# Four heads written out, another order at the heads' ends, and finer waits around the output projection, in a hybrid block on one core

## The reference

```python
def mlstm_branch(...):
    xc = jax.nn.silu(causal_conv(xm, conv_w, conv_b))
    q, k = heads(xc) @ w_q, (heads(xc) @ w_k) * MLSTM_HEAD_DIM ** -0.5
    v = heads(xm) @ w_v
    h = mlstm_chunkwise(q, k, v, i_pre, logf)
    h = jax.nn.sigmoid(heads(z)) * h
    mu, var = mean(h), mean((h - mu) ** 2)          # over the 384 of a head
    h = (h - mu) * lax.rsqrt(var + EPS)
    h = h * mh_gain + skip * xc
    return h @ w_proj
...
    merged = jax.nn.sigmoid(g_a) * y_a + jax.nn.sigmoid(g_b) * y_b
    h = h + merged @ w_out[l]
    h = h + peer(rmsnorm(h, norm2_g[l]), w_query[l], ...)
```

## Time and profile before

| | us |
|---|---|
| median of 3 runs | 4103.37 (4101.56 to 4104.65) |
| the profiled execution | 4104.21 |
| its span, first to last instruction | 4102.7 |
| PE busy | 3998.3 (97%) |
| DVE, ACT, POOL busy | 2465.8, 1239.6, 939.0 |
| granted clock of the PE, mean | 0.990 |
| a matmul of 128x128 by 128x512, mean (2048 of them, L1889) | 0.391 |

### The profile page before, as it was taken

One profiled execution on the slowest core, in us unless ns is written; L12 is line 12 of the kernel. 1 busy time (PEld: TensorE's weight loads), 2 busy tenths in 40 slices (PEclk: granted clock), 3 DMA queues, 4 the chain that ended last, 5 costly groups with the idle time before them and its releaser, 6 DMA issues.

```text
span 4102.7 us, 54068 instructions
## 1 busy us (share of the span) xinstructions
PE 3998.3 (97%) x19149; PEld 3450.3 (84%) x19149; DVE 2465.8 (60%) x3452; ACT 1239.6 (30%) x1313; POOL 939.0 (23%) x679
## 2 busy tenths in 40 slices
PE   8999999988999899999999999999999999999997
PEld 5887777776778688888888888888899999999997
DVE  7556777466532745454666664222247887888884
ACT  4333232333222422222333332222222222222223
POOL 3100000421111254545000000000014444444432
PEclk9999999999999999999999999999999999999999
DMA  4643333642543445455777778666768888888883
GB/s 173 197 140 123 127 123 113 228 151 77 179 146 115 165 157 183 159 183 187 229 252 239 243 238 307 218 216 215 228 225 301 322 301 313 306 308 323 303 321 127
DMA packets 239995, 867.64 MB, mean 211 GB/s; under 512 B 22680, under 2 KB 61096, under 8 KB 172224
## 3 DMA queue, kind: packets, MB, share of 16 engines
q1 hardware_dynamic: 96576, 454.07, 30.5%
q10 hardware_dynamic: 94080, 204.49, 16.2%
q0 software_dynamic: 49280, 208.36, 14.4%
HBM read 768.25 MB, written 232.81 MB: 244 GB/s over the span
## 4 chain that ended last, share of the span: by engine, by line
PE 50%; DVE 6%; DMA 5%; issue 3%; ACT 2%; DVEq 1%; SPq 0%; ACTq 0%
PE mm L1889 12%; PE mm L1890 12%; PE mm L1891 12%; DMA raw<-stream 5%; DVE wlo L1101 2%; PE pv L1889 2%; PE pv L1890 2%; PE pv L1891 2%; DVE acc L1813 2%; PE sc L1891 1%; PE sc L1890 1%; PE sc L1889 1%; ACT whi L673 1%; ACT actb L1009 1%; DVE gl L1788 1%
## 5 line engine op out<-in xcount | busy, mean ns | idle before, releaser
L1101 DVE TENSOR_TENSOR wlo<-raw,whi 128x2048 fp32r<-128x2048 f32 x331 | 759.2, 2294 | 773.3 <-ACT whi L673 763.6
L673 ACT ACTIVATE whi<-raw 128x2048 fp32r<-128x2048 f32 x380 | 727.5, 1914 | 493.0 <-issue 194.2
L1889 PE MATMUL mm<-t_hi,whi 128*128 128x512 f32 x2048 | 800.0, 391 | 7.5 <-DVE t_lo L1618 3.9
L1890 PE MATMUL mm<-t_lo,whi 128*128 128x512 f32 x2048 | 798.0, 390 | 0.0
L1891 PE MATMUL mm<-t_hi,wlo 128*128 128x512 f32 x2048 | 797.6, 389 | 0.0
L1889 PEld LDWEIGHTS mm<-t_hi,whi 128*128 128x128 f32 x2048 | 385.1, 188 | 90.5 <-DVE t_lo L1618 8.1
L1891 PEld LDWEIGHTS mm<-t_hi,wlo 128*128 128x128 f32 x2048 | 384.7, 188 | 80.7
L1890 PEld LDWEIGHTS mm<-t_lo,whi 128*128 128x128 f32 x2048 | 385.1, 188 | 77.6
L1889 PE MATMUL mm<-hn_hi,whi 128*128 128x512 f32 x960 | 377.4, 393 | 4.6 <-DVE wlo L1101 4.6
L1890 PE MATMUL mm<-hn_lo,whi 128*128 128x512 f32 x960 | 374.3, 390 | 0.0
L1891 PE MATMUL mm<-hn_hi,wlo 128*128 128x512 f32 x960 | 373.8, 389 | 0.0
...
## 6 DMA issues: line engine op xcount, KB each, us to landing
...
ev_d<-stream ACTq DMA_DIRECT2D x128, 1024.0 KB, 6.1
up_d<-sgl ACTq DMA_DIRECT2D x128, 256.0 KB, 2.1
...
gg<-g_d SPq DMA_DIRECT2D x15, 1536.0 KB, 12.2
gl<-up_d SPq DMA_DIRECT2D x120, 192.0 KB, 5.1
...
```

Of the source, the lines that this page charges most:

```text
L673: act.activation(whi[:, k, :], raw[:, k, :], ACT.Copy).then_inc(hi_done, 1)
L1101: dve.tensor_tensor(wlo[:, k, :], raw[:, k, :], whi[:, k, :].bitcast(F32), ALU.subtract)\
L1889: pe.matmul(out, lh, rh, start=start, stop=False)
L1890: pe.matmul(out, lh, rl, start=False, stop=False)
```

## The change

Heads: all four are written out on every engine, with no loop. DVE writes the divided sums to a new buffer `gh`, which POOL gates in place; the centring reads `gh` and writes `hh`. So a head's tail now spreads over two heads: the mean, centring, squares and root of head h-1 in head h; its gain, skip and halves in head h+1. The low half is written by POOL (`finished_low`), for the last head by DVE. DVE does both units' `wlo` and the Newton step ahead of the division. The PE does `qk(4)` ahead of the mean, and the squares after `value(1)`. The third square has a buffer of its own (`hs2`). POOL issues `m_bc` and `gcol` before the gating, `em_bc` after it, beside `sz`.

Before the heads: within the GLU loop POOL loads four instead of eight late blocks of `xc`; the others go in one piece behind the first `xm`.

Roots: one `Abs_reciprocal_sqrt` in place of Ln and Exp, in all places; the Newton step stays.

Output projection: its first tile waits for 15 merged blocks, and for the 16th only at its end. The last tile signals each block, on which ScalarE writes `t_hi`; DVE does 13 blocks of `t_lo` before the last residual. The sum of squares goes into the first query tile, before its sixth block.

```diff
-        gcol = S("gcol", [P, TB], F32, 200)
+        gcol = S("gcol", [P, TB], F32, 207.25)
+        gh = S("gh", [P, HC, T], F32, 152)
+        hs2 = S("hs2", [P, T], F32, 200)
...
-        hsq = (hs[:, 0, :], hs[:, 1, :], pf[:, 0, :])
+        hsq = (hs[:, 0, :], hs[:, 1, :], hs2[:])
...
-                c = MC - KC // 2 + p
-                load_conv(1, slice(c, c + 1))
+                if p < HC + 1:
+                    load_conv(1, slice(HC + 1 + p, HC + 2 + p))
...
+            def finished_low(h):
+                for c in range(HC):
+                    pool.wait_ge(hfhi_done, 3 * h + c + 1)
+                    pool.tensor_tensor(xc_lo[:, 3 * h + c, :], hh[:, c, :], xc_hi[:, 3 * h + c, :].bitcast(F32),
+                                       ALU.subtract).then_inc(hflo_done, 1)
...
-            def head(h, first, last):
-                if not first:
-                    z_gate(h - 1)
-                    pool.wait_ge(en_done, 4 * h)
-                    pool.wait_ge(pv_free, 3 * h)
-                    pool.dma_start(m_bc[:], gates_d[1, h].partition_broadcast(P)).then_inc(bcst_in, 16)
-                    pool.dma_start(em_bc[:], gates_d[2, h].partition_broadcast(P)).then_inc(bcst_in, 16)
-                    with nc.allow_non_contiguous_dma(reason="one value a partition"):
-                        pool.dma_start(gcol[:], gates_d[0, h].rearrange("(s p) -> p s", p=P)).then_inc(bcst_in, 16)
+            def next_gates(h):
+                pool.wait_ge(en_done, 4 * h)
+                pool.dma_start(m_bc[:], gates_d[1, h].partition_broadcast(P)).then_inc(bcst_in, 16)
+                with nc.allow_non_contiguous_dma(reason="one value a partition"):
+                    pool.dma_start(gcol[:], gates_d[0, h].rearrange("(s p) -> p s", p=P)).then_inc(bcst_in, 16)
+            def next_sz(h):
                 pool.wait_ge(hz_done, 3 * h)
                 pool.dma_start(sz[:], z_heads[h]).then_inc(sz_in, 16)
-                if not first:
-                    skips(h - 1, (0, 1))
-                if not last:
+                if h:
+                    pool.wait_ge(pv_free, 3 * h)
+                    pool.dma_start(em_bc[:], gates_d[2, h].partition_broadcast(P)).then_inc(sz_in, 16)
+            next_xm(0)
+            load_conv(1, slice(MC - HC - 1, MC))
+            next_sz(0)
+            next_xm(1)
+            for h in range(1, HEADS):
+                next_gates(h)
+                z_gate(h - 1)
+                next_sz(h)
+                if h >= 2:
+                    skips(h - 2, (2,))
+                    finished_low(h - 2)
+                if h < HEADS - 1:
                     next_xm(h + 1)
-                if not first:
-                    skips(h - 1, (2,))
-            next_xm(0)
-            head(0, True, False)
-            with pool.Fori(1, HEADS - 1) as h:
-                head(h, False, False)
-            head(HEADS - 1, False, True)
+                skips(h - 1, (0, 1))
             z_gate(HEADS - 1)
...
-                act.activation(rs[:], ms[:], ACT.Ln).then_inc(ln_done, 1)
-                act.wait_ge(ln_done, r + 1 + (HEADS if r else 0))
-                act.activation(rs[:], rs[:], ACT.Exp, scale=-0.5).then_inc(rt_done, 1)
+                act.activation(rs[:], ms[:], ACT.Abs_reciprocal_sqrt).then_inc(rt_done, 1)
...
                     act.activation(p_hi[:, s, P * s:T], pf[:, s % 2, 0:T - P * s], ACT.Copy).then_inc(phi_done, 1)
-                qkv(0)
-                qkv(1)
-                qkv(2)
-                qkv(3)
-                if not first:
-                    tail_squares(h - 1)
+                for j in range(5):
+                    qkv(j)
                 weights(0)
                 weights(1)
-                qkv(4)
                 qkv(5)
-                if not first:
-                    tail_root(h - 1)
+                if h >= 2:
+                    tail_high(h - 2, hh)
                 qkv(6)
+                if h:
+                    tail_squares(h - 1, hh)
                 weighted_high(0)
                 qkv(7)
                 weights(2)
+                if h:
+                    tail_root(h - 1)
                 weighted_high(1)
                 qkv(8)
                 weights(3)
...
                 split_hi(U_QKV // 2 + h + 1, 0, (proj_done, O_QKV + 10 * h + 10))
                 weighted_high(3)
                 split_hi(U_QKV // 2 + h + 1, 1)
-                if not first:
-                    tail_high(h - 1)
...
+            next_hi(U_HEAD // 2 - 1, 0, (proj_done, O_UP - 2))
+            residual_square(KC // 2 - 1, 0)
+            next_hi(U_HEAD // 2 - 1, 1, (proj_done, O_UP - 1))
             g2 = vec[:, V_G2:V_G2 + KC]
+            def scaled_high(d):
+                act.activation(t_hi[:, d, :], h2[:, d, :], ACT.Copy, scale=g2[:, d:d + 1]).then_inc(ahi_done, 1)
+            for d in range(KC - 1):
+                act.wait_ge(proj_free, O_WO + d + 1)
+                act.wait_ge(u3_done, KC - 1 + d + 1)
+                scaled_high(d)
+            residual_square(KC // 2 - 1, 1)
             act.wait_ge(proj_done, O_UP)
-            for d in range(KC):
-                act.wait_ge(proj_free, O_WO + d + 1)
-                act.activation(t_hi[:, d, :], h2[:, d, :], ACT.Copy, scale=g2[:, d:d + 1]).then_inc(ahi_done, 1)
-                if d == 7:
-                    next_hi(U_HEAD // 2, 0, (proj_done, O_UP))
+            scaled_high(KC - 1)
+            next_hi(U_HEAD // 2, 0, (proj_done, O_UP))
             root(1)
...
-                    dve.scalar_tensor_tensor(hh[:, c, :], st[:], -1.0 / HD, hh[:, c, :], ALU.mult, ALU.add)\
+                    dve.scalar_tensor_tensor(buf[:, c, :], st[:], -1.0 / HD, gh[:, c, :], ALU.mult, ALU.add)\
...
-                qkv(0)
-                qkv(1)
-                qkv(2)
-                qkv(3)
-                if not first:
-                    centre(h - 1)
-                dve.wait_ge(bcst_in, 48 * h + 48)
+                for j in range(4):
+                    qkv(j)
+                if h >= 2:
+                    gain(one, h - 2, hh)
+                    skip(h - 2, 0, hh)
+                    skip(h - 2, 1, hh)
+                dve.wait_ge(bcst_in, 32 * h + 48)
                 exponent(0)
+                qkv(4)
                 exponent(1)
-                qkv(4)
-                if not first:
-                    variance(h - 1)
+                if h >= 2:
+                    skip(h - 2, 2, hh)
                 qkv(5)
+                if h:
+                    dve.wait_ge(hflo_done, 3 * (h - 1))
+                    centre(h - 1, hh)
                 qkv(6)
                 weighted(0)
                 exponent(2)
                 weighted_low(0)
                 qkv(7)
+                if h:
+                    variance(h - 1)
                 weighted(1)
                 exponent(3)
                 weighted_low(1)
                 qkv(8)
                 weighted(2)
-                if not first:
-                    scale(one, h - 1, last)
                 weighted_low(2)
                 qkv(9)
                 weighted(3)
                 weighted_low(3)
                 split_lo(U_QKV // 2 + h + 1, 0)
-                if last:
-                    finish(one, h - 1)
-                    split_lo(U_QKV // 2 + h + 1, 1)
+                split_lo(U_QKV // 2 + h + 1, 1)
+                if h:
+                    scale(one, h - 1)
                 dve.wait_ge(den_done, h + 1)
+                if h:
+                    dve.wait_ge(sz_in, 32 * h + 16)
                 one(dve.scalar_tensor_tensor(rd[:], dn[:], -1.0, em_bc[:], ALU.mult, ALU.max))
                 one(dve.tensor_tensor(rd[:], dn[:], rd[:], ALU.max))
                 one(dve.reciprocal(rd[:], rd[:]))
-                if not last:
-                    split_lo(U_QKV // 2 + h + 1, 1)
-                    if not first:
-                        finish(one, h - 1)
-                dve.wait_ge(hflo_done, 3 * h)
                 for c in range(HC):
                     dve.wait_ge(pv_done, 3 * h + c + 1)
-                    dve.tensor_tensor(hh[:, c, :], heads_out[c][:], rd[:], ALU.mult).then_inc(pv_free, 1)
+                    dve.tensor_tensor(gh[:, c, :], heads_out[c][:], rd[:], ALU.mult).then_inc(pv_free, 1)
...
+            scaled_low(range(KC - 3))
+            residual(KC // 2 - 1, 1)
+            scaled_low(range(KC - 3, KC))
+            next_lo(U_HEAD // 2, 0)
...
                 qk(3)
+                qk(4)
                 if not first:
                     mean(h - 1)
-                qk(4)
-                if not first:
-                    squares(h - 1)
                 qk(5)
                 pe.wait_ge(xm_in, 32 * h + 32)
                 value(0)
                 pe.wait_ge(proj_free, o + 6)
                 scores(0)
-                for s in (1, 2, 3):
+                value(1)
+                if not first:
+                    squares(h - 1)
+                scores(1)
+                for s in (2, 3):
```

(23 more changed lines are left out.)

127 lines of the change are left out of this document (67 added, 60 removed).

## The result

| | before | after |
|---|---|---|
| device time, median (range), 4 runs each | 4104.0 us (4101.6 to 4105.4) | 4079.3 us (4077.8 to 4081.5) |
| ratio | | 0.9941, 95% interval 0.9924 to 0.9958 |
| profiled execution, time and span | 4104.2, 4102.7 us | 4077.8, 4076.2 us |

A forecast was written before the change was run, and what follows sets the result against it. PE waits and the slow-clock matmuls after them were taken to bound the kernel. Terms 2 + 2.3 + 4.0 + 4.9 + 7 + 5.3 + 6.4 + 1.9 = 33.8, say 34 us, gave 4069 us, range 4055 to 4086.

The forecast's parts named there:

- the last root: Last norm: a table load and an activation leave the path, 1.9 us won; by the skill's figure 3.3.
- the end of the projection: Output projection's end: blocks follow one by one and the root comes earlier, 6.4 us won, bounds 3 and 9.
- the tail: After the four heads: early weights and gates, centring from S4+14.7, 7 us won, bounds 5 and 8.
- sign of being wrong: Wrong if heads 2 and 3 stay over 44 us, or query 0 waits over 5 us for the sum of squares.
- Projection's front: Output projection's start: the last merged block's 3.4 us wait and its 1.9 cold part go, 5.3 us won.
- Heads 2 and 3: Attention heads: gating wait goes, smaller waits at q_lo and squares come; 4.0 and 4.9 us won, bounds 2 and 6 each.
- DVE's start into the weights' low halves: Heads 2 and 3: DVE starts the first wlo at S-4.1, S being the PE's first matmul of a head.
- The rule on POOL and DVE: Heads 2 and 3: SBUF operations of the two exclude each other; by it the sum is 2 us smaller.
- Head 0: First head: two xc loads ahead of xm go, shortening the xm_lo wait; 2 us won, bounds minus 1 and plus 5.
- Written-out heads: Heads without a loop: some 500 more PE instructions, fewer register operations; nothing taken, bounds 0 and minus 3.
- The clock did not stay down: Rival in the heads: several shorter waits keep the clock at 1.2 GHz, 4144 us with half the stage cold; chance 0.05.
- Rival 1: Heads 1 to 3 and projection's end: new waits as large as the old, 19 us won, 4084; chance 0.09.

The follow-up runs named there:

- kernel 2: The changed kernel with the second sum of squares put back behind the whole of query 0, instead of before block 5; 4079.0 us.
- kernel 5: The changed kernel with the low halves of heads 0 to 2 made by DVE instead of POOL; 4075.1 us.
- kernel 1: The changed kernel with the six roots put back to a logarithm and an exponential; 4082.0 us.
- kernel 6: The changed kernel with the Newton steps of a head's root moved behind the next head's division and first four low halves, before the gain; 4078.5 us.
- kernel 12: The changed kernel without head 2's finishing in the tail (gain, skips, high and low halves left out); 4074.4 us.
- kernel 11: kernel 8 plus POOL adding head 3's blocks during DVE's reciprocal, squares behind scores(2), weights split first at two merged blocks; 4059.5 us.
- kernel 8: The changed kernel with DVE's head order rearranged, low halves on DVE, earlier centring and variance in the tail, second sum of squares at block 10; 4068.8 us.
- kernel 10: The changed kernel with the four late conv chunks (2 MB) held back until the PE is at head 0's sixth block; 4081.9 us.

## Why the prediction was right, and where it was not

**In short:** the direction, the range and the places of the gain were right, and 24.1 of the 33.8 us came. Every term but the last root and the end of the projection fell short, most of all the tail, so the total was not saved by errors that cancel; only the size of the term of the projection's end was right by luck. The high bounds add up to 44, not 46, so 4059 should stand for the 4057; nothing hangs on it.

**What bounds the kernel** was read rightly: PE waits and their cold matmuls in one stage, all else unchanged. Every new wait that was named came, in its place: `q_lo` at K tile 1, ScalarE's `hs` at the squares (1.13 in heads 2 and 3, against 1.4), DVE 3.7 us for POOL's `xc_lo` (against 4), the sum of squares (3.10, against 3.3), none on `mg_lo` and none over 0.7 on the gates. Neither sign of being wrong appeared: heads 2 and 3 stay under 44 us (43.2 and 43.4), and the sum of squares is waited for less than 5 us. The first normalised low half came at T+19.5 (against T+19.9).

**Projection's front and end, last root:** right in size. Behind the end's 6.8 us the reasoning was partly wrong, and the size right by luck: it credited the early root, but kernel 2 shows that the root was of no use there and its sum cost 2.0 us (0.4 where the clock stayed up, in kernel 5), and kernel 1 that one activation less gained nothing at this place. The step that failed is "what is gained is the root". For the last root the prediction had two figures, 1.9 from the rows and 3.3; it measured 1.94.

**Heads 2 and 3, 6.3 won and not 8.9.** The mis-sized step is DVE's start into the weights' low halves, set at S-4.1 because the Newton steps had gone from among the weighting. DVE was not busy there: it waits for the last `p_lo`, whose chain over PE and ScalarE did not move. It started at S-2.5, so the `q_lo` wait is 3.3 and 3.5 instead of 1.6 to 2.1, and cold matmuls follow it. That the chain behind it is DVE's queue is shown by kernel 6 (2.6 us less work ahead: wait 0.6 and 0.9).

**Tail, 1.7 won and not 7.** This is over half of the miss. The step said that DVE does head 2's gain and skips "meanwhile" and centres at S4+14.7. It put them at their durations with POOL idle. Beside POOL's gating and low halves the three gains took 4.20 us and not 2.07, the third skip 1.73 and not 0.75, and the centring started at S4+17.1; and the squares on the PE, cold behind a 5.0 us wait, took 4.5 us, of which the term had half. The Newton start came at S4+25.4 instead of 19.6 to 20.5, and from there the old 9.9 us held. Kernel 12 shows the whole price of the work that was moved in, with the cold matmuls that it brings: 7.1 us. Before the change it stood beside head 3, and the prediction looked at the waits that left the tail more than at the work that came in.

**The rule on POOL and DVE** was weighed, and put at 2 us in the heads, but left out of the tail, where it counts most. The rows now say more: beside POOL, DVE operations that read two tiles in SBUF are held (0.69 to 1.64), those with one input in PSUM are not (two `q_lo` in 1.28 beside the gating), nor is the reciprocal (3.35 beside POOL's additions in kernel 11). For the heads, kernel 5 shows the price: POOL's low halves cost 1.4 and 0.4 us there. The Trainium skill (SBUF — State Buffer, SBUF: two separate sides) says that the engine that starts first holds the shared ports for the whole instruction; by it a held operation pays up to one POOL step, 1.24 us, and the trace agrees, with 0.95 us in one `TENSOR_TENSOR` of kernel 8. The one-input `TENSOR_SCALAR` (0.43 to 1.37) is held too. The Trainium skill, in the same section, says this of operations in a two-port mode; whether this is one, no run here shows.

**Head 0, 0.5 won and not 2.** The term took the whole transfer time of the two loads ahead, 1.6 us, off the wait, but the landing fell only from 9.1 to 8.5 us. Why it does not fall further is open: kernel 10 excludes the late chunks. Issuing the `xm` loads ahead of the wait for `ya_out` wasn't tried, since their place in SBUF is still in use.

**Written-out heads:** head 1 is PE work alone now, 36.58 of 36.58 us busy (1.7 us won and not 2.3, since PE work alone had been put at 35.9), and no wait at a head's start appeared. Whether the loop had cost anything by itself wasn't tried.

**Rivals.** The clock did not stay down (heads 2 and 3 went from 0.93 and 0.89 to 0.96). Rival 1, waits as large as the old ones, went halfway: the `q_lo` wait was some 1.5 us longer than worked out, but left heads 2 and 3 two thirds of their gain.
